# The attention of a hybrid decoder step on one core: products with V as fp16 halves instead of fp32

## The reference, cut to what matters

```python
logits = jnp.einsum('bqgrd,bqkgd->bqgrk', qg, kg).astype(jnp.float32) * (HEAD_DIM ** -0.5)
...
p = jax.nn.softmax(logits, axis=-1).astype(vg.dtype)
o = jnp.einsum('bqgrk,bqkgd->bqgrd', p, vg)
```

## Time and profile before

| | |
|---|---|
| median of three executions | 4145.21 us |
| the profiled execution: time | 4125.75 us |
| the profiled execution: span in the trace | 4124.0 us |
| PE busy | 3360.2 us, 81% of the span |
| DVE busy | 2155.6 us, 52% |
| ACT busy | 1862.1 us, 45% |
| POOL busy | 1533.3 us, 37% |
| mean granted TensorE clock | 0.89 of full speed |

### The profile page before, as it was taken

How to read it: one execution, slowest core, us unless ns; L and a number is a source line. 1 busy time by engine, 2 the same in 40 slices (tenths; PEclk the granted TensorE clock), 3 DMA queues, 4 the chain that set the end, 5 groups by cost and what they waited for, 6 DMA issues and landing times.

```text
span 4124.0 us, 57250 instructions
## 1 busy us (share of the span) xinstructions
PE 3360.2 (81%) x20090; PEld 1862.5 (45%) x20090; DVE 2155.6 (52%) x3955; ACT 1862.1 (45%) x2780; POOL 1533.3 (37%) x1100
## 2 busy tenths in 40 slices
PE   6953696699977968799888977799969866999765
PEld 2542354244446452344376451344457742444355
DVE  3627564799025628799144628699963431200145
ACT  1322234555445336554464336554355524453356
POOL 0031103478531023676421022576521014675323
PEclk8985698899989999899999999899989967999856
DMA  2201021133320311232210310232310153232256
GB/s 89 92 15 41 16 95 35 52 101 97 93 76 11 97 38 51 67 102 89 69 62 1 95 42 26 66 100 90 96 34 1 54 164 117 87 100 84 90 186 214
DMA packets 112067, 313.09 MB, mean 76 GB/s; under 512 B 14034, under 2 KB 20514, under 8 KB 111746
## 3 DMA queue, kind: packets, MB, share of 16 engines
q1 hardware_dynamic: 111874, 310.63, 24.0%
HBM read 296.35 MB, written 14.24 MB: 75 GB/s over the span
## 4 chain that ended last, share of the span: by engine, by line
PE 57%; DVE 18%; issue 9%; ACT 5%; DMA 3%; POOLq 3%; POOL 2%; DVEq 2%; ACTq 0%; SPq 0%
PE bank L567 14%; PE bank L568 14%; PE bank L569 14%; DVE spare L1310 7%; PE bank L806 5%; DVE scores L1542 3%; PE bank L795 2%; ACT ring L961 1%; DVE ring L1278 1%; DMA kT<-in_w_gu 1%; DVE R L1596 1%; DVE miss L1313 1%; POOL H L1816 1%; PE bank L781 1%; PE bank L887 1%
## 5 line engine op out<-in xcount | busy, mean ns | idle before, releaser
L567 PE MATMUL bank<-H,ring 128*128 128x512 f16 (+2 forms) x2560 | 860.8, 353 | 188.1 <-POOL H L1816 92.8
L568 PE MATMUL bank<-H,ring 128*128 128x512 f16 (+2 forms) x2560 | 861.5, 353 | 0.0
L569 PE MATMUL bank<-H,ring 128*128 128x512 f16 (+2 forms) x2560 | 860.6, 353 | 0.0
L1310 DVE TENSOR_SCALAR_CACHE_REDUCE spare<-scores,cand 128x640 uint8<-128x640 f32 (+4 forms) x448 | 662.5, 1479 | 43.4 <-issue 3.6
L1708 POOL TENSOR_TENSOR ring<-raw,ring 128x1024 f16<-128x1024 f32 (+1 forms) x252 | 488.7, 1940 | 339.6 <-ACT raw L963 339.2
L961 ACT ACTIVATE ring<-raw 128x1024 f16<-128x1024 f32 (+2 forms) x356 | 349.1, 981 | 373.7 <-PE bank L569 275.5
L567 PEld LDWEIGHTS bank<-H,ring 128*128 128x128 f16 (+1 forms) x2560 | 259.9, 102 | 468.0 <-issue 175.3
L569 PEld LDWEIGHTS bank<-H,ring 128*128 128x128 f16 (+1 forms) x2560 | 262.4, 103 | 249.9 <-issue 14.2
L1596 DVE CUSTOM_DVE_ANT_0 R<-bank,scores 128x512 f32<-128x512 f32 (+3 forms) x256 | 140.9, 592 | 446.1 <-PE bank L783 436.9
L568 PEld LDWEIGHTS bank<-H,ring 128*128 128x128 f16 (+1 forms) x2560 | 260.7, 102 | 240.5 <-issue 6.8
L567 PE MATMUL bank<-R,ring 128*128 128x512 f16 (+1 forms) x880 | 296.1, 352 | 37.5 <-POOL R L1837 25.5
(11 more groups left out here) (293 smaller groups left out, 6037.6 us busy)
## 6 DMA issues: line engine op xcount, KB each, us to landing
raw<-in_w_gu SPq DMA_DIRECT2D x132, 512.0 KB, 3.6
raw<-in_w_in SPq DMA_DIRECT2D x104, 512.0 KB, 3.6
kT<-in_w_gu SPq DMA_DIRECT2D x88, 512.0 KB, 3.8
raw<-in_w_d SPq DMA_DIRECT2D x48, 384.0 KB, 3.1
X<-in_xT SPq DMA_DIRECT2D x8, 2048.0 KB, 9.0
raw<-in_w_d SPq DMA_DIRECT2D x48, 320.0 KB, 2.9
raw<-in_w_out SPq DMA_DIRECT2D x24, 512.0 KB, 3.5
kT<-in_w_d SPq DMA_DIRECT2D x32, 384.0 KB, 3.2
```

What stands on the lines that cost most here:

```text
L567: mm(o, lhs[0], rhs[0], start=first, stop=False)
L568: mm(o, lhs[0], rhs[1], start=False, stop=False)
L569: return mm(o, lhs[1], rhs[0], start=False, stop=last)
L1310: v.tensor_scalar(flags[:, 0:128 * (i + 1)], row_of(i), cut_at[:, i % 4:i % 4 + 1], None, ALU.is_ge, ALU.add, accum_out=tally[:, i % 4:i % ...
```

## The change

V is kept as two fp16 numbers, high and low, whose sum is V times 16. For each token and each of the two KV heads `vtok` now holds [high | low], 2 x 64 columns, in as many bytes as before. ACT writes the projected V to a scratch area `v32`; DVE makes both halves of it once for each block, in phase P (two TENSOR_SCALAR and two SCALAR_TENSOR_TENSOR), and the store of V to memory reads `v32`.

The probabilities are kept in the same way. ACT's `copy_pT` writes the high half, fp16, with a factor 4096; DVE reads the same PSUM bank again and writes the low half (`low_pT`), in the queue behind `mask` of the next unit and ahead of `lows` and `scale`. A new semaphore `a_pTl` counts these, and PE's `turn` and `values` wait for it where they waited for `a_pTc`.

`values` does two fp16 matmuls for each key tile, high and low probabilities, each against the 128 columns [high | low] of V of the head's group. The head's output is the sum of the two halves of the columns, so `scale` becomes two instructions with a drain between them. The factors are taken out in `copy_mix`.

```diff
-        vtok = sb("vtok", [128, SEQ // 128, 128])
+        vtok = sb("vtok", [128, SEQ // 128, KVH, 2, HD], F16)
+        v32 = cut(Rf, 10752, 4, 128)
-        pT = cut(Rf, 4096, 2, 16, 128)
+        pT = cut(Rf, 4096, 4096).bitcast(F16).rearrange("p (u t s n) -> p u t s n", u=2, s=2, n=128)
...
                             if n >= 2:
-                                pe.wait_ge(S("a_pTc"), n - 1)
+                                pe.wait_ge(S("a_pTl"), n - 1)
...
                     def values(i, h):
                         u = 8 * i + h
-                        pe.wait_ge(S("a_pTc"), TN[i, h, -(-(i + 1) // 4) - 1] + 1)
+                        pe.wait_ge(S("a_pTl"), TN[i, h, -(-(i + 1) // 4) - 1] + 1)
                         if u >= 2:
                             pe.wait_ge(S("a_scaled"), u - 1)
 
                         for t in range(i + 1):
-                            last = mm(bank[5 + u % 2][:, 0:128], pT[:, u % 2, t, :], vtok[:, t, :],
-                                      start=(t == 0), stop=(t == i))
+                            for half in range(2):
+                                last = mm(bank[5 + u % 2][:, 0:128], pT[:, u % 2, t, half, :],
+                                          vtok[:, t, h // 4, :, :].rearrange("p s n -> p (s n)"),
+                                          start=(t == 0 and half == 0), stop=(t == i and half == 1))
...
-                            A(pT[:, u % 2, 4 * g:4 * g + w, :],
+                            A(pT[:, u % 2, 4 * g:4 * g + w, 0, :],
                               bank[3 + n % 2][:, 0:128 * w].rearrange("p (t n) -> p t n", n=128),
-                              ACT.Copy).then_inc(S("a_pTc"), 1)
+                              ACT.Copy, scale=P_UP).then_inc(S("a_pTc"), 1)
...
+                        if u == 22 and b < NBLK:
+
+                            dve.wait_ge(S("p_copied"), out_counts(b, TILES.index(("v", 0)))[0])
+                            v4 = v32.rearrange("p t (g n) -> p t g n", g=KVH)
+                            for g in range(KVH):
+                                v.tensor_scalar(vtok[:, 4 * b:4 * b + 4, g, 0, :], v4[:, :, g, :], V_UP, None, ALU.mult)
+                            dve.drain()
+                            for g in range(KVH):
+                                v.scalar_tensor_tensor(vtok[:, 4 * b:4 * b + 4, g, 1, :], v4[:, :, g, :], V_UP,
+                                                       vtok[:, 4 * b:4 * b + 4, g, 0, :], ALU.mult, ALU.subtract)
...
-                        v.tensor_scalar(osb[:, i % 2, 64 * h:64 * h + 64], bank[5 + u % 2][:, 64 * (h // 4):64 * (h // 4) + 64],
-                                        rden[:, u % 4:u % 4 + 1], None, ALU.mult).then_inc(S("a_scaled"), 1)
+                        o, r = osb[:, i % 2, 64 * h:64 * h + 64], rden[:, u % 4:u % 4 + 1]
+                        v.tensor_scalar(o, bank[5 + u % 2][:, 64:128], r, None, ALU.mult)
+                        dve.drain()
+                        v.scalar_tensor_tensor(o, bank[5 + u % 2][:, 0:64], r, o, ALU.mult, ALU.add
+                                               ).then_inc(S("a_scaled"), 1)
+
+                    def low_pT(i, h, groups):
+
+                        u = 8 * i + h
+                        for g in range(-(-(i + 1) // 4))[groups]:
+                            n = TN[i, h, g]
+                            dve.wait_ge(S("a_pTc"), n + 1)
+                            w = min(4, i + 1 - 4 * g)
+                            hi, lo = (pT[:, u % 2, 4 * g:4 * g + w, half, :] for half in range(2))
+                            v.scalar_tensor_tensor(lo, bank[3 + n % 2][:, 0:128 * w].rearrange("p (t n) -> p t n", n=128),
+                                                   P_UP, hi, ALU.mult, ALU.subtract).then_inc(S("a_pTl"), 1)
...
                     for n in range(len(units)):
                         if n + 1 < len(units):
                             mask(*units[n + 1])
+                        low_pT(*units[n], slice(None))
                         if n in WEIGHT_UNITS:
```

More of the change, by code:

```diff
@@ L65 @@
 W_UP, H_UP, M_UP, U_UP = 256.0, 64.0, 16.0, 4.0
+V_UP, P_UP = 16.0, 4096.0
 WT = KT * 128
@@ L263, in layer @@
         rep = cut(ikT[:, :, :].rearrange("p s n -> p (s n)").bitcast(F32), 0, DB, 64)
-        cache = [vtok[:, :, :].rearrange("p (g t) n -> p g (t n)", g=NPG),
+        cache = [vtok[:, :, :, :, :].rearrange("p t g s n -> p (t g s n)").bitcast(F32).rearrange(
+                     "p (g n) -> p g n", g=NPG),
                  near_bias[:, :, :].rearrange("p (g h) n -> p g (h n)", g=NPG),
@@ L466, in _ @@
                         pairs.append((a["o_v"][t0:t0 + NT].rearrange("(t p) n -> p t n", p=128),
-                                      vtok[:, 4 * b:4 * b + 4, :]))
+                                      v32))
                     else:
@@ L1047, in _ @@
                         elif what == "v" and b < NBLK:
-                            dst, src = vtok[:, 4 * b:4 * b + 4, :], o[:, :].rearrange("p (t c) -> p t c", c=128)
+                            dst, src = v32, o[:, :].rearrange("p (t c) -> p t c", c=128)
                         elif what == "v":
@@ L1146, in copy_mix @@
                         src = bank[7][:, :].rearrange("p (j n) -> p j n", n=128)
-                        A(mix32, src, ACT.Copy, scale=M_UP)
-                        A(mixA[:, 0, :, 128 * (i % 4):128 * (i % 4) + 128], src, ACT.Copy, scale=M_UP
+                        A(mix32, src, ACT.Copy, scale=M_UP / (P_UP * V_UP))
+                        A(mixA[:, 0, :, 128 * (i % 4):128 * (i % 4) + 128], src, ACT.Copy, scale=M_UP / (P_UP * V_UP)
                           ).then_inc(S("a_mix"), 1)
```

## The result

The changed kernel takes 4200.84 us, median of four executions (4183.44 to 4214.89); the kernel before, beside it, 4145.09 us (4142.46 to 4157.85). The ratio is 1.0126, with an interval of 1.0072 to 1.0181: slower. A second set, run later (experiment e9), gave 4190.6 against 4138.73 us, ratio 1.0131, 1.0098 to 1.0165.

A forecast was written before the change was run, and what follows sets the result against it. TensorE was taken to set the pace in the last three phases A, VectorE in the first. Terms +12.2, +18.7, +11.9, -5.6, +17.4 make +54.6 on 4125.75 us (4180); medians lie 19.5 higher: 4200 us, range 4160 to 4240.

The forecast's parts named there:

- PE's saving: In the product with V, two fp16 matmuls cost 0.112 instead of 0.224 us a key tile; 1.68 in tile 14.
- the rival of a spacing of 0.112: In the product with V, fp16 halves don't shorten TensorE's time: +53 us, 4253; chance 2%.
- The ring: Tiles 8 to 15: mask, exponential, copy, low half, `scale`, mask form a closed loop; 7.96 us in tile 14.
- The loop's terms: Times a head: tiles 4 to 7, VectorE's own work, 2.93 to 3.81 us; tiles 8 to 15, loop, 4.57 to 8.19.
- The units with `turn_out`: `turn_out` waits for a `scale` that comes last, and the next mask for it: 1.3 us, three times in the last phase.
- The sum by phase: Phases A, first to last exponential: first +17.4 us, second +11.9, third +18.7, last +12.2.
- the unknown costs: Low half's spacing, -14 to +12 us; weight units and `turn_out`, -35 to +17; own range 4165 to 4232 us.
- Cheap low halves: Low halves cheap or beside waits, so no difference: at half price +6 us, about 4151; chance 9%.
- PE's saving passes through: Tiles 4 to 15 save 113 us, less 17 in the first phase: faster, 4050 us; chance 3%.
- The clock falls: TensorE at half clock in a quarter of the last three phases A adds 53 us: 4253; chance 10%.
- signs of being wrong: Low half well under 0.6 us, TensorE last waited for in tiles 12 to 15, or late-phase clock under 0.9.
- What was costed at nothing: Splitting V in phases P, covered by TensorE's work (7 us if not), and ACT's copies with a scale, unchanged.

The follow-up runs named there:

- e9: The changed kernel run once more, unedited: 4190.6 us, ratio to the kernel before 1.0131.
- e4: The changed kernel without the low halves of the probabilities, TensorE doing as many products: 4053.43 us, ratio to the kernel before 0.9805.
- e2: The changed kernel with low halves of the first two groups of tiles 8 to 15 made twice: phases A 862.4 us against 858.1.
- e3: The changed kernel with low halves of the third and fourth groups of tiles 8 to 15 made twice: phases A 915.2 us against 858.1.
- e1: The changed kernel with `scale` of the unit two before moved ahead of the low halves: 4133.2 us, ratio to the kernel before 0.996.
- The filler: The changed kernel with groups of 12 fp16 matmuls, results unread, where TensorE would wait: 4180.54 us, ratio to the kernel before 1.0103.
- e10: The changed kernel with the same unread matmuls, run again on the same chip as e9: 4189.32 us, ratio to the kernel before 1.0124.

## Why the prediction was right, point by point

**PE's saving.** Forecast 0.112 us a key tile; measured 1.67 us for 15 (3.51 to 1.84). Right. The Trainium skill's stream of about 81 ns (TensorE: Matmul & The Clock Gate, Back-to-back issue gap) doesn't hold here; the spacing is 0.056 us. With it the rival of a spacing of 0.112 fails.

**The ring.** Right in kind in tiles 8 to 15: ACT's copy of group 3 stands directly behind the exponential, DVE waits for it (60.6 us in the last phase) and no longer for PE (6.6 us against 107.8). e4, e2 with e3, and e1 each moved one link, and the time followed.

**The loop's terms.** All slightly too long:

| tile | 4 | 5 | 6 | 8 | 9 | 11 | 12 | 13 | 14 | 15 |
|---|---|---|---|---|---|---|---|---|---|---|
| forecast | 2.93 | 3.20 | 3.54 | 4.57 | 5.04 | 6.47 | 6.86 | 7.11 | 7.96 | 8.19 |
| measured | 2.66 | 2.94 | 3.27 | 4.35 | 4.83 | 6.24 | 6.54 | 6.78 | 7.64 | 7.87 |

Tiles 7 and 10 are left out, since their heads in after don't settle at one value for long. In tile 14 the mask to exponential is exact (3.26). The excess of 0.32 is: exponential to copy 0.02; hand-over from copy to low half, 0.03 and not 0.08; two low halves 1.07 and not 1.25, since an instruction starts some 0.09 us before the end of the one ahead; `scale` to mask 0.80 and not 0.87, for the same reason. The prediction named this as the lower bound of its unknown (0.61 us spacing, -14 us) and took 0.69.

**The units with `turn_out`.** Forecast 1.3 us more each, nine times. In the last phase the three took 10.05, 11.27 and 11.62 us instead of 8.48, 7.79 and 8.12. That is 8.55 more, 7.7 without the growth of the heads around them, against 3.9. This is a term mis-sized the other way: the transpositions and logits in it were priced at full clock, and ran at half after the wait. The filler, which keeps the clock up there, takes 4.8 us off the three (e10 against e9). Five heads of that phase, too, took longer than their neighbours, by 5.1 us together (7.87, 7.22 and 7.21 in tile 12, 8.74 in tile 14, 9.22 in tile 15); the product of the last of them took 3.54 us for 32 instead of 1.95. Heads as in the table and `turn_out` as forecast would have given 229 us for the phase and not 244.6. These two causes make 9 of the difference; the other 7, in the units with a weight tile and around them, I haven't taken apart.

**The sum by phase**, between the first and last exponentials. The rows of after, which answer to the earlier trace rows:

```profile
L1131 ACT ACTIVATION_READ_ACCUMULATOR R<-R,nmax x32: 185/186/211, 329.9 to 497.4; 128x1 f32 x32
L1131 ACT ACTIVATION_READ_ACCUMULATOR R<-R,nmax x32: 185/187/202, 1235.0 to 1349.8; 128x1 f32 x32
L1131 ACT ACTIVATION_READ_ACCUMULATOR R<-R,nmax x32: 185/191/202, 2119.9 to 2303.0; 128x1 f32 x32
L1131 ACT ACTIVATION_READ_ACCUMULATOR R<-R,nmax x32: 186/199/203, 3099.8 to 3344.4; 128x1 f32 x32
```

First 167.5 us, +17.1 (forecast +17.4); second 114.8, +7.1 (+11.9); third 183.1, +19.0 (+18.7); last 244.6, +18.0 (+12.2). In the first the heads grew by 0.57, 0.69 and 0.83 us, each some 0.09 less than forecast, and one early unit by 2.5 us, which was not foreseen. With the ends of the phases, +54.6 us in one profile and +51.4 in the other, against +54.6. That the sum was met to the microsecond is in part luck: heads too dear by 0.2 to 0.3 us, and clock and `turn_out` too cheap, cancelled. By phase the forecast was 4.8 us too high in the second and 5.8 too low in the last. The range of 4165 to 4232 doesn't follow from the unknown costs beside it, either: their bounds, -14 and -35, +12 and +17, added to 4200 give 4151 to 4229.

**The rivals.** "Cheap low halves" failed: they cost 130 us. "PE's saving passes through" was forecast at 4050 us, and e4 measures 4053.43 once they are gone. The closeness is partly chance: forecast were 113 us less in tiles 4 to 15 and 17 more in the first phase, and the phases A of e4 are 81.2 shorter in the last three and 5.7 longer in the first. "The clock falls" was given as all or nothing and came in part: 0.92, 0.92 and 0.89 in the last three phases, instead of 0.96 to 0.97; the filler gave back some 10 us of it. One of the forecast's signs of being wrong, a clock under 0.9 in the last three phases, did show: 0.89 in the last of them. PE was also busier than forecast in phases A: 72 to 75% and not some 65%. How long one wait was doesn't tell where the clock fell. The lower clock was there after waits of PE's matmuls of 2.78 us (e3) and 2.41 us (`turn_out`); the waits of 2.02 us in each head of tile 14 mostly left it high. In the last phase of after it stayed at full level through two waits of 3.43 us, of which one is shown, and in tile 15 it fell after one of 1.64 (the unit before had waited 2.04):

```profile
3149.01 0.28 PE L784 MATMUL bank<-kT,q 128*128 128x256 f16 x1 [3.43 <-DVE mx L1611]
...
3149.24 1.04 PE L798 MATMUL bank<-cst,R 128*128 128x128 f32 x8
...
3322.93 0.28 PE L784 MATMUL bank<-kT,q 128*128 128x256 f16 x1 [1.64 <-DVE mx L1611]
...
3324.69 3.54 PE L810 MATMUL bank<-vtok,R 128*128 128x128 f16 x32
...
3333.86 1.95 PE L810 MATMUL bank<-vtok,R 128*128 128x128 f16 x32
```

The granted clock from 3143 to 3153 us, around the first wait, was 1.00; from 3324.6 to 3328 it was 0.50.

**What was costed at nothing.** The split of V takes 2 x 0.29 and 2 x 0.42 us a block, and a cost in the phases P can't be told from their spread (+3 us in sum in one profile, 0 in the other). ACT's copies with a scale last what they did (0.98 to 1.09 for two).

## What to carry to other kernels

Work taken off the busiest engine is worth nothing while what replaces it stands between a late producer and the next thing that engine needs: here the low halves took back the 75 us that e4 shows, and 55 more. Before pricing such an instruction, ask for its place: much the same work cost 4 us ahead of the awaited copy (with a better clock in its favour) and 57 behind it. In a queue, put what waits for nothing (`scale`, two units old) ahead of what waits; and look for the form of the product whose result needs no second pass, as three products of 64 columns did here.

## What the runs showed of the hardware

PE's clock fell inside a loop of short waits, after waits of 1.64, 2.41 and 2.78 us, and stayed up through two of 3.43; what PE ran at the lower level took up to nearly twice as long (1.91 us for eight transpositions instead of 1.04, 3.54 for a product instead of 1.95). A whole phase G of 42 us at clock 0.96 took 58 us at 0.57 in some executions, of the same kernel too: 58.3 us in the first profile of after, 43.1 us at 0.92 in e9. 64-column fp16 matmuls, each with its own weights, follow each other by 0.029 us, those of 128 columns by 0.056: time goes with columns down to this size. DVE's instructions from PSUM start about 0.09 us before the end of the one ahead, so a pair of 0.69 us costs 0.60 each when nothing waits between them.
